# Spreads that pick one row out of 128: full-height matmuls in place of 8-row and 4-row ones

## The reference, cut to what matters

```
c = jnp.cumsum(logf, axis=1)                       # logf: log-forget value per token and head
s = jnp.einsum('bqhd,bkhd->bhqk', qb, k) * (dh ** -0.5)
s = s + cb[..., None] - c_keys[:, :, None, :]      # minus the key's sum: one row, the same for all queries
...
def mix_by_denominator(outs, lses):
    w = jax.nn.softmax(jnp.stack(lses, axis=0), axis=0)
    o = jnp.sum(w[..., None] * jnp.stack(outs, axis=0).astype(jnp.float32), axis=0)
```

## Time and profile before

| what | value |
|---|---|
| median of 3 runs | 2865.83 us (2865.34 to 2872.45) |
| profiled execution | 2871.23 us, its span 2869.2 us |
| PE busy | 2807.9 us (98%) |
| loads of weights (PEld) | 1905.6 us (66%) |
| DVE, ACT, POOL busy | 1026.5, 528.5, 142.2 us |
| the chain that ended last | PE 94%, DMA 3%, DVE 1%, issue 1%, SP queue 1% |

### The profile page before, as it was taken

How to read it: one execution, slowest core, us unless ns; L and a number is a source line. 1 busy time by engine, 2 the same in 40 slices (tenths; PEclk the granted TensorE clock), 3 DMA queues, 4 the chain that set the end, 5 groups by cost and what they waited for, 6 DMA issues and landing times.

```text
span 2869.2 us, 37948 instructions
## 1 busy us (share of the span) xinstructions
PE 2807.9 (98%) x14500; PEld 1905.6 (66%) x14500; DVE 1026.5 (36%) x2631; ACT 528.5 (18%) x1159; POOL 142.2 (5%) x267
## 2 busy tenths in 40 slices
PE   8999999999999999999999999998999999999998
PEld 7655556777655555466544567447888888878887
DVE  2155553232253233233221123345666666610002
ACT  2133322221201112111111111321111111100001
POOL 0000001020101122100000000000000000000000
PEclk9999999999999999999999999998999999999999
DMA  4000101100117678765602300533354441141101
GB/s 184 22 12 9 57 1 54 56 18 21 43 26 200 200 220 249 241 189 177 233 0 88 118 30 30 182 103 106 124 179 139 150 150 48 42 141 44 41 1 63
DMA packets 198569, 285.99 MB, mean 100 GB/s; under 512 B 20637, under 2 KB 136494, under 8 KB 197350
## 3 DMA queue, kind: packets, MB, share of 16 engines
q1 hardware_dynamic: 139558, 179.10, 19.3%
q10 hardware_dynamic: 42976, 89.39, 9.7%
q0 software_dynamic: 15856, 15.07, 2.2%
HBM read 259.55 MB, written 63.35 MB: 113 GB/s over the span
## 4 chain that ended last, share of the span: by engine, by line
PE 94%; DMA 3%; DVE 1%; issue 1%; SPq 1%; ACT 0%; ACTq 0%; DVEq 0%
PE psum L2379 20%; PE psum L2653 11%; PE psum L939 10%; PE psum L1844 8%; PE psum L1928 7%; PE psum L515 5%; PE psum L2081 4%; PE psum L686 3%; PE psum L1267 3%; PE psum L702 3%; PE psum L1852 3%; PE psum L1303 2%; PE psum L1283 2%; PE psum L713 2%; PE psum L2055 2%; DMA arena<-in_cache_fox_kv 1%
## 5 line engine op out<-in xcount | busy, mean ns | idle before, releaser
L2379 PE MATMUL psum<-arena 128*128 128x272 f32 x2464 | 567.8, 394 | 0.0
L2379 PEld LDWEIGHTS psum<-arena 128*128 128x128 f32 x2464 | 470.0, 191 | 97.4
L2653 PE MATMUL psum<-arena 128*128 128x256 f32 (+1 forms) x1760 | 327.6, 360 | 6.7 <-DVE arena L2682 6.7
L939 PE MATMUL psum<-arena 128*128 128x512 f32 (+3 forms) x960 | 316.9, 481 | 1.4 <-ACT arena L568 1.4
L2653 PEld LDWEIGHTS psum<-arena 128*128 128x128 f32 (+1 forms) x1760 | 288.0, 180 | 45.5 <-DVE arena L2682 7.0
L1844 PE MATMUL psum<-arena 128*128 128x368 f32 (+1 forms) x768 | 305.9, 499 | 1.7 <-ACT arena L1880 1.1
L1928 PE MATMUL psum<-arena 128*128 128x512 f32 x512 | 238.3, 599 | 0.8 <-issue 0.8
L939 PEld LDWEIGHTS psum<-arena 128*128 128x128 f32 (+1 forms) x960 | 194.9, 250 | 62.4 <-issue 35.1
L762 DVE CUSTOM_DVE_ANT_0 arena<-psum,arena 128x256 f32<-128x256 f32 (+2 forms) x224 | 95.2, 457 | 214.0 <-PE psum L686 213.8
L1844 PEld LDWEIGHTS psum<-arena 128*128 128x128 f32 x768 | 125.4, 193 | 68.4 <-issue 46.3
L2482 DVE TENSOR_TENSOR arena<-arena,psum 128x272 f32<-128x272 f32 (+2 forms) x330 | 113.4, 377 | 157.9 <-PE psum L2379 157.1
(11 more groups left out here) (221 smaller groups left out, 2740.6 us busy)
## 6 DMA issues: line engine op xcount, KB each, us to landing
arena<-in_cache_fox_kv SPq DMA_DIRECT2D x128, 256.0 KB, 4.2
arena<-in_cache_fox_kv ACTq DMA_DIRECT2D x128, 256.0 KB, 4.3
out_win_s<-in_cache_win_kv ACTq DMA_DIRECT2D x8, 4080.0 KB, 14.8
arena<-in_w_up SPq DMA_DIRECT2D x44, 512.0 KB, 6.1
arena<-in_cache_win_kv SPq DMA_DIRECT2D x16, 1024.0 KB, 8.0
arena<-in_cache_mem_kv SPq DMA_DIRECT2D x16, 1024.0 KB, 6.9
arena<-in_w_in SPq DMA_DIRECT2D x9, 1024.0 KB, 7.8
arena<-in_w_down SPq DMA_DIRECT2D x3, 2816.0 KB, 11.7
```

Source lines behind the costliest of these rows:

```text
L939: last = pe.matmul(banks[c0 // 512][p0:p0 + r, 0:n], xn_tile(k, g, t), wD[g][:, k, w0:w0 + n], start=(k == 0), stop=(k == KD - 1))
L2379: last = pe.matmul(banks[n % 8][:, 0:Q4], w[:, k, :], r[:, k, Q4 * p:Q4 * p + Q4], start=(k == 0), stop=(k == 3))
L2653: last = pe.matmul(banks[u % 2][p0:p0 + r, 0:n], hT(f)[:, t * P:t * P + r], wd[q % 2][:, f, c0:c0 + n], start=(f == 0), stop=(f == NF - 1))
```

## The change

The forget-sum spread reads all 128 rows of the identity's column and all 128 partitions of `cT`; the column is zero but for one row. For that `cT` is cleared as a whole by POOL at the start (one more memset, 128 by 1024), and VectorE waits for the clears before it writes its 8 rows. The spread of the dilated weights takes columns of the identity too: each of the 12 becomes two matmuls of 128 rows by 64 columns, one for the upper and one for the lower half of the bank's partitions, the same moving operand for both. For that VectorE clears the whole of `stT`'s weight part (128 by 3 by 512) where before it cleared 36 partitions of one group. The table `head_rows` goes, so the tables that are loaded have 960 columns and not 1216; the 256 columns stay reserved (`spare`), so that all other addresses are as before. ScalarE's first wait is for one clear and not for four.

```diff
@@ -79,11 +79,6 @@
         for j in range(NS):
             a[b * NS:b * NS + j + 1, b, j] = -1
     c["new_sum"] = a.reshape(P, -1)
-    sel = np.zeros((P, 2, P))
-    for hh in range(HD):
-        sel[hh, hh // 2, 64 * (hh % 2):64 * (hh % 2) + 64] = 1
-        sel[32 + hh] = sel[hh]
-    c["head_rows"] = sel.reshape(P, -1)
     inv = np.float32(10000.0) ** (-np.arange(32, dtype=np.float32) / np.float32(32))
     for g in range(NG):
         tab = np.zeros((P, TT, 2, 32))
@@ -101,7 +96,7 @@
 
 
 CONST_COLS = [("ident", 128), ("ones", 128), ("upto", 128), ("after", 128), ("band_mask", 256),
-              ("pair_mask", 128), ("new_sum", 64), ("head_rows", 256)]
+              ("pair_mask", 128), ("new_sum", 64)]
 
 
 def make_sample_tables():
@@ -220,6 +215,7 @@
             cst[n] = cst_all[:, col:col + w]
             col += w
         ident, ones = cst["ident"], cst["ones"]
+        spare = take(256)
         G_NAMES = ("g_mix", "g_xattn", "g_mem", "g_ffn")
         gcols = take(4 * KD)
         gT = {n: gcols[:, KD * i:KD * (i + 1)] for i, n in enumerate(G_NAMES)}
@@ -245,7 +241,7 @@
         s_crow = sem("conv_rows_loaded")
         s_vecT = sem("vectors_turned")
         s_vec = sem("vectors_kept")
-        s_clear = sem("block_diagonals_cleared")
+        s_clear = sem("regions_cleared")
         stats_all = take(96 * NG, f0 + 6144 + 192)
         vrows = take(4 * P, f0).rearrange("p (a c) -> p a c", a=4)
         grows = take(4 * P, f0 + 512).rearrange("p (a c) -> p a c", a=4)
@@ -257,7 +253,7 @@
                 act.dma_start(grows[0:KD, n, :], src).then_inc(s_grow, 16)
             act.dma_start(bfg, I["b_fgate"][0:1, :].partition_broadcast(P)
                           .rearrange("p o h -> p (o h)")).then_inc(s_bfg, 16)
-            act.wait_ge(s_clear, 4)
+            act.wait_ge(s_clear, 1)
             act.activation(std[:, TT * 5 - 1:TT * 5], eps_t, ACT.Sqrt)
 
         def conv_rows_sp(sp):
@@ -270,6 +266,7 @@
             pool.memset(stats_all, 0.0).then_inc(s_clear, 1)
             pool.memset(qbF, 0.0).then_inc(s_clear, 1)
             pool.memset(qbD, 0.0).then_inc(s_clear, 1)
+            pool.memset(cT, 0.0).then_inc(s_clear, 1)
 
         def prep_pe(pe):
             pe.wait_ge(s_tab, 16)
@@ -471,6 +468,7 @@
                                      in1=lft[:, 1, :], op0=ALU.min, op1=ALU.subtract).then_inc(fp["lf_out"], 1)
             yield at("sums")(1)
             dve.wait_ge(fp["summed"], 1)
+            dve.wait_ge(s_clear, 5)
             dve.tensor_copy(cT[0:HF, :], psum[0:HF, 3 * 512:5 * 512]).then_inc(fp["sums_out"], 1)
 
         def forget_sums_pe(pe):
@@ -498,8 +496,8 @@
                     if j == 0 and n == 0:
                         pe.wait_ge(fp["sums_out"], 1)
                     pe.wait_ge(fp["copied"], q - 1)
-                    pe.matmul(banks[q % 2], ident[0:HF, 2 * j + n // 2:2 * j + n // 2 + 1].to_broadcast([HF, P]),
-                              cT[0:HF, n % 2 * 512:(n % 2 + 1) * 512], start=True, stop=True).then_inc(fp["computed"], 1)
+                    pe.matmul(banks[q % 2], ident[:, 2 * j + n // 2:2 * j + n // 2 + 1].to_broadcast([P, P]),
+                              cT[:, n % 2 * 512:(n % 2 + 1) * 512], start=True, stop=True).then_inc(fp["computed"], 1)
                     continue
                 w, (c0, cw) = (wK if kind == "k" else wQ), CHUNKS[n]
                 for k in range(KD):
@@ -1110,8 +1108,11 @@
                     m = n * NG + g
                     if m >= 4:
                         pe.wait_ge(cb["product"], m - 3)
-                    pe.matmul(banks[3 + m % 4], cst["head_rows"][32 * c:32 * c + HD, j * P:(j + 1) * P],
-                              stT[32 * c:32 * c + HD, g, 0, :], start=True, stop=True).then_inc(cb["spread"], 1)
+                    for a in range(2):
+                        row = 32 * c + 2 * j + a
+                        last = pe.matmul(banks[3 + m % 4][64 * a:64 * a + 64, :], ident[:, row:row + 1].to_broadcast([P, 64]),
+                                         stT[:, g, 0, :], start=True, stop=True)
+                    last.then_inc(cb["spread"], 1)
 
         def combine_act(act):
             yield at("combine")(0.5)
@@ -1124,8 +1125,9 @@
                 yield now(0.12 * g + 0.03)
                 if g == 0:
                     att_over(dve, att_dil[NG - 1])
-                    dve.memset(stT[0:RH, 2, 0, :], 0.0)
+                    dve.memset(stT[:, :, 0, :], 0.0).then_inc(s_clear, 1)
                     dve.memset(stT[0:RH, 2, 1, :], 1.0)
+                    dve.wait_ge(s_clear, 6)
                 dve.wait_ge(cb["turned"], g + 1)
                 for a in range(2):
                     if g == 0:
```

## The result

The changed kernel takes 2852.52 us (median of 7 executions, 2846.26 to 2858.98) against 2865.34 (7 executions, 2860.49 to 2872.45). The ratio is 0.995, with a 95% interval from 0.993 to 0.997: 12.8 us faster, where 20.3 were forecast. Two more sets of the same kernel gave 2852.98 against 2863.80 and 2851.07 against 2866.24. One execution of the kernel before in a later set, 4474.65 us at a mean granted clock of 0.591, is left out of all medians. The profiled execution took 2858.98 us, against 2871.23 before.

A forecast was written before the change was run, and what follows sets the result against it. TensorE (PE), busy 98% of the span, was taken as the bound. Gains of 14.6 + 1.5 + 3.9 + 0.3 = 20.3 us, subtracted from the median 2865.8, gave 2845.5 us; range 2837 to 2864.

The forecast's parts named there:

- Part 1: Front, forget-sum spreads: 128 rows end 30.72 us of half clock; 14.6 us gained after 0.8 of added waits.
- Part 2: Front, borders between 8-row and 128-row matmuls: 12 go, at 0.1 to 0.2 us each; 1.5 us gained, bounds 0 and 2.4.
- Part 3: Combine stage: paired 64-column spreads cost nothing extra and half clock goes; 3.9 us gained, bounds 0 and 6.8.
- both rivals with pairs in turn: Combine stage: pairs run in turn, at full clock 10.3 us more, 2856 (4%); at half clock +31 us, 2880 (4%).
- Part 4: Kernel start and clears: larger clears are covered; the smaller table load gains 0.3 us, bounds 0 and 1.1.
- rival "not by rows": Spreads: clock goes by values at work or something coinciding, so half clock stays; 2864 us; chance 13%.
- partly lost gain: Page stages: half-clock stretches may shift, each costing 1.7 us per 3.4; three or four give 2852, within the forecast's range.

The follow-up runs named there:

- the wider products: Changed kernel with 84 of the sample's 96 branch-product matmuls streaming 128 columns, not 64: 2848.65 and 2848.52 us, against 2852.98 and 2851.07 for the changed kernel.

## Why the prediction was right in kind and too large in size

**Part 1, the clock behind the forget-sum spreads: right, but its size was one execution's.** In the profiled pair the front gave 15.9 us where parts 1 and 2 said 16.1. The added wait for ScalarE's copy was 0.5 us and not 0.8; this is the changed kernel's, where 0.5 stood before:

```profile
PE psum L711 <- ACT arena L740: 1.0, 4, 0.3
```

The range held, and 2852.5 lies 7.0 us above the 2845.5 of the sum; the range had been stretched to 2864 to take in a rival, so that it held says little. The step that failed is the sum against the median. I took the 30.72 us of half clock from one profile and subtracted the gain, whole, from the median of other executions. The mean of four profiles with 8 rows is 23.0 us, worth 11.5 us and not 15.4. The mean clock told it: 0.986 in that execution, a median of 0.989 over 29. The three times shown ahead of the forecast, 2865.34 to 2872.45, already told that the profiled 2871.23 was at the slow end, and I treated the 5.4 us as a constant when they were part of the very term that I was pricing.

**Part 2, the borders: nearer 1.0 us than 1.5, and read from the wrong gap.** The 0.76 us of idle loader were taken as the price of a change of shape, but the row puts them down to ScalarE's copy (L558). In the changed kernel, where no shape changes at this place, the loader still waits for that copy:

```profile
129.83 0.30 PEld L513 LDWEIGHTS psum<-arena 128*128 128x128 f32 x2 [0.58 <-ACT arena L556]
```

What the border adds is the difference, 0.18 us, and the first cluster takes 3.61 us on the chain for 3.71 before. Over the whole front the 15.9 us, less the clock's 15.4 and with the 0.5 us of added wait, leave an estimate of 1.0 us for the borders, from one pair of profiles.

**Part 3, the combine stage: right.** 4.7 us where 3.9 were forecast; at the last product, which the page loads wait for, it is 4.0 (it starts at 844.47 for 862.94 us). The pairs are side by side, so both rivals with pairs in turn fall. "TensorE: Matmul & The Clock Gate" in the Trainium skill, Part 3, "The mechanism", says that each 32-by-32 tile of the array can compute on a different output slice and that such tiles overlap. This trace agrees for two halves that share one moving operand (12 in 2.79 us). The 2.9 us that PE gains behind the last product are mostly lost in the wait for the first page, as counted: the shift falls from -21.4 us at the last gate matmul (847.28 for 868.64 us) to -19.2.

**Part 4, small things: the 0.3 us are not there.** The clears were covered, as counted (that of `cT` ended at 3.2 us; VectorE's took 1.34 us, and 3.83 us of its idle time were left). But b_fgate did not land sooner. The tables' 480 KB took 5.1 to 5.4 us to land in the six profiles that load them, where 608 KB took 5.3 to 5.4 in the other eight, and the step of VectorE that waits for b_fgate starts at 9.62 to 10.69 us, three times above 10.3, against 9.55 to 9.78. Why it comes late in some is open. The forget sums start at 99.9, 98.7 and 100.2 us in the three profiles of the changed kernel and at 98.6, 100.1 and 99.2 in those of before, so the 1.4 us by which PE is behind here are scatter as much as anything.

**The rival "not by rows": refuted.** With 120 or more of the 128 partitions at zero the clock stayed at 1.00 through the whole front. "TensorE: Matmul & The Clock Gate" in the Trainium skill, Part 1, "What's actually happening", says that the gate goes by how busy the PE has been recently. The runs show that this can't be read as the time in which matmuls are in flight: with 8 rows and with 128 PE is busy alike (199.25 and 199.00 of 200 us), and only the first loses the clock.

**The partly lost gain: it happened.** I had it as stretches of 1.7 us that may shift, within the forecast's range. It was one long stretch at loader-bound matmuls, 8.1 us. In the profiled executions it is most of what is missing: 15.9 + 4.7 - 1.4 - 8.1 = 11.1, with 1.0 more behind it makes the 12.0 of the spans. In the median both causes share. Estimates are 3.9 us for the half clock that the usual execution of before doesn't have (15.4 against 11.5), and up to the 3.8 us that the wider products brought; together they are near the 7.5 us by which 12.8 falls short of 20.3. No run takes them apart in the median.

## What to carry to other kernels

Look at the granted clock stretch by stretch, and at the rows that the matmuls ahead of a drop read: a matmul that picks one row out of 8 takes as long itself as one over 128 partitions, of which 127 are multiplied by zero (587 and 592 ns), and the full one keeps the clock for what follows. Before a gain of clock is priced, take the half-clock time from several executions, or from the mean clock of many; the one profile here held 30.7 us where the mean of four is 23.0. Where loads of weights set the pace, more moving columns can be free and can keep the clock (the 96 instructions took 10.90 us with 64 and with 128 columns here).

## What the runs showed of the hardware that I had not expected

- Rows of zeros count for the clock: with 64 rows of which 56 are zero the clock from 120 to 320 us is 1.00, with 8 it is 0.92 to 0.96.
- Height seems to work by degree: 17 to 31 (four profiles), 3 to 7 (two), and 0 us of half clock with 8, 32 and 64 rows.
- The time at full clock is steady: over 29 executions of 2854.5 to 2877.6 us the span less half of the half-clock time stays within 2826.4 to 2834.6, with a mean of 2830.5 us, so most of the scatter of this kernel is TensorE's clock.
- A run of short matmuls can stay at half clock with PE busy nearly throughout: the stretch of 23.9 us, PE busy for 23.06, takes in the branch products from 1381.17 us on and the first 6 us of full-size ones behind them. The same run with twice the moving columns in 84 of 96 had 1.00.
